# Summing the sample heads' state products: two float32 products with a selector, or two turns on TensorE and a VectorE sum

## The reference, cut to what matters

```python
s = jnp.einsum('bhtd,bhsd->bhts', q, k) * w_ts
decay = jnp.exp(b + m_prev[..., None] - m_t)
num = decay[..., None] * jnp.einsum('bhtd,bhdv->bhtv', q, c_prev) + jnp.einsum('bhts,bhsv->bhtv', s, v)
den = decay * jnp.einsum('bhtd,bhd->bht', q, n_prev) + jnp.sum(s, axis=-1)
h = num / jnp.maximum(jnp.abs(den), jnp.exp(-m_t))[..., None]
...
c_new = carry[..., None, None] * c_prev + jnp.einsum('bhs,bhsd,bhsv->bhdv', g, k, v)
```

## Time and profile before

| what | value |
|---|---|
| median of 3 runs | 1702.03 us |
| the profiled execution, its own time | 1702.65 us |
| its span in the trace | 1700.9 us |
| TensorE matmul busy | 1690.0 us, 99% |
| VectorE busy | 1199.5 us, 71% |
| ScalarE busy | 766.8 us, 45% |
| GpSimd busy | 478.9 us, 28% |
| mean granted TensorE clock | 0.998 of full speed |

### The profile page before, as it was taken

The page is one execution under the profiler, slowest core; times in us unless marked ns, Lnnn a source line. Parts: engine busy times, 40 slices in busy tenths (PEclk is TensorE's granted clock), DMA queues, the critical chain, the costliest instruction groups (busy, mean ns, idle before and its releaser), DMA issues.

```text
span 1700.9 us, 37193 instructions
## 1 busy us (share of the span) xinstructions
PE 1690.0 (99%) x13726; PEld 1683.3 (99%) x13726; DVE 1199.5 (71%) x1901; ACT 766.8 (45%) x916; POOL 478.9 (28%) x501
## 2 busy tenths in 40 slices
PE   9999999999999999999999999999999999999997
PEld 8999999999999999999999999999999999999997
DVE  5875958668495866849688877777555777777554
ACT  6534435454443535444445555544333434334443
POOL 4432515232151523215333222222000222222220
PEclk9999999999999999999999999999999999999999
DMA  8788786868778686877776666666666666666663
GB/s 199 185 232 196 196 215 153 231 164 227 185 201 207 155 232 161 232 181 201 194 183 180 191 176 184 181 178 174 183 181 180 182 179 181 177 181 178 184 176 120
DMA packets 591165, 318.80 MB, mean 187 GB/s; under 512 B 17684, under 2 KB 585988, under 8 KB 588988
## 3 DMA queue, kind: packets, MB, share of 16 engines
q1 hardware_dynamic: 578564, 292.99, 64.0%
q10 hardware_dynamic: 10448, 21.57, 4.7%
q0 software_dynamic: 2064, 2.92, 0.8%
HBM read 305.09 MB, written 12.78 MB: 187 GB/s over the span
## 4 chain that ended last, share of the span: by engine, by line
PE 99%; ACT 0%; POOL 0%; DVE 0%; issue 0%; ACTq 0%; POOLq 0%; DVEq 0%
PE strip L1532 32%; PE strip L1524 32%; PE strip L1528 32%; PE aux L1403 1%; PE aux L1411 1%; PE strip L1455 0%; PE aux L1585 0%; PE aux L1475 0%; PE strip L1468 0%; PE aux L1615 0%; PE aux L1614 0%; PE aux L1628 0%; PE strip L1403 0%; PE aux L1619 0%; PE aux L1620 0%; PE aux L1612 0%
## 5 line engine op out<-in xcount | busy, mean ns | idle before, releaser
L982 DVE TENSOR_TENSOR w_lo<-w_raw,w_hi 128x1024 fp32r<-128x1024 f32 x556 | 720.4, 1299 | 309.3 <-ACT w_hi L713 308.7
L713 ACT ACTIVATE w_hi<-w_raw 128x1024 fp32r<-128x1024 f32 x557 | 586.5, 1059 | 751.8 <-PE strip L1532 710.2
L1524 PE MATMUL strip<-xh,w_hi 128*128 128x268 f32 (+1 forms) x2016 | 291.1, 286 | 0.0
L1532 PE MATMUL strip<-xh,w_lo 128*128 128x268 f32 (+1 forms) x2016 | 290.7, 286 | 0.0
L1528 PE MATMUL strip<-xl,w_hi 128*128 128x268 f32 (+1 forms) x2016 | 290.1, 286 | 0.0
L1532 PEld LDWEIGHTS strip<-xh,w_lo 128*128 128x128 f32 x2016 | 265.2, 188 | 0.4
L1524 PEld LDWEIGHTS strip<-xh,w_hi 128*128 128x128 f32 x2016 | 265.1, 188 | 0.2
L1528 PEld LDWEIGHTS strip<-xl,w_hi 128*128 128x128 f32 x2016 | 265.3, 188 | 0.0
L1524 PE MATMUL strip<-x2h,w_hi 128*128 128x266 f32 x1408 | 200.1, 284 | 0.0
L1528 PE MATMUL strip<-x2l,w_hi 128*128 128x266 f32 x1408 | 199.9, 284 | 0.0
L1532 PE MATMUL strip<-x2h,w_lo 128*128 128x266 f32 x1408 | 199.9, 284 | 0.0
(11 more groups left out here) (330 smaller groups left out, 1529.1 us busy)
## 6 DMA issues: line engine op xcount, KB each, us to landing
w_raw<-in_w_in SPq DMA_DIRECT2D x256, 512.0 KB, 4.5
w_raw<-in_w_up SPq DMA_DIRECT2D x176, 512.0 KB, 4.1
w_raw<-in_w_down SPq DMA_DIRECT2D x64, 512.0 KB, 4.0
w_raw<-in_w_out SPq DMA_DIRECT2D x32, 512.0 KB, 4.4
w_raw<-in_w_down SPq DMA_DIRECT2D x32, 384.0 KB, 3.4
out<-c_st ACTq DMA_DIRECT2D x8, 1024.0 KB, 7.0
c_st<-in_state_mlstm_C ACTq DMA_DIRECT2D x7, 1024.0 KB, 11.2
rb<-scratch_rows ACTq DMA_DIRECT2D x8, 270.0 KB, 5.1
```

The costliest lines, as they stand in the source:

```text
L713: act.activation(w_hi[:, slot, :], w_raw[:, slot, :], ACT.Copy).then_inc(hi_done, 1)
L982: v.tensor_tensor(w_lo[:, slot, :], w_raw[:, slot, :], w_hi[:, slot, :].bitcast(f32), ALU.subtract).then_inc(lo_done, 1)
L1524: pe.matmul(bank[b][:, 0:c1 - c0], w_hi[:, slot, w], rh[:, k0 + k, c0:c1], start=(first and k == 0), stop=False)
L1532: mm = pe.matmul(bank[b][:, 0:c1 - c0], w_lo[:, slot, w], rh[:, k0 + k, c0:c1], start=False, stop=(last and k == kk - 1))
```

## The change

The two products with `sel` become two turns of the halves of `sacc` (128 x 128 each, in one pass) into `aux0` and `aux1`, columns 258 to 385. VectorE then sums the 16 groups with two `tensor_reduce` into `hsum` (128 x 2 x 8) at `i` 22, ahead of the multiplication into `h_t`, and waits for its own two results. `sel`, the instruction that makes it and the semaphore for it are gone. `hsum` has 64 bytes on each partition, `sel` had 32.

```diff
-        sel = sb("sel", [P, NS])
+        hsum = sb("hsum", [P, 2, NS])
...
-            v.tensor_reduce(sel[:, :], ident[:, :].rearrange("p (g b) -> p b g", b=NS), mybir.AxisListType.X, ALU.add)\
-             .then_inc(sel_done, 1)
...
                         v.wait_ge(sample_done, n + 1)
-                        v.tensor_tensor(h_t[:, :, PM:NM], aux[0][:, PM:PM + 2 * NS].rearrange("p (a b) -> p a b", a=2),
+                        for w in range(2):
+                            v.tensor_reduce(hsum[:, w, :], aux[w][:, PM:PM + P].rearrange("p (g b) -> p b g", b=NS),
+                                            mybir.AxisListType.X, ALU.add).then_inc(hsum_done, 1)
+                        v.wait_ge(hsum_done, n * 2 + 2)
+                        v.tensor_tensor(h_t[:, :, PM:NM], hsum[:, :, :],
                                         rden[:, PM:NM].unsqueeze(1).broadcast_to([P, 2, NS]), ALU.mult)\
                          .then_inc(hs_step, 1)
...
-                        pe.wait_ge(sel_done, 1)
                         pe.wait_ge(sacc_step, (n + 1) * (JG + 1))
                         for w in range(2):
-                            mm = pe.matmul(aux[0][:, PM + w * NS:PM + (w + 1) * NS], sacc[:, 0, w * P:(w + 1) * P],
-                                           sel[:, :], start=True, stop=True)
+                            mm = turn(aux[w][:, PM:PM + P], sacc[:, 0, w * P:(w + 1) * P], P)
                         mm.then_inc(sample_done, 1)
```

More of the change, by code:

```diff
@@ L328, in hybrid_decoder_step @@
             sem("scores_done"), sem("kv_turned"), sem("kv_done"), sem("vs_done"), sem("v_kept"))
-        wsc_done, qkd_done, qkd_turned, sn_done, sel_done = (
-            sem("wsc_done"), sem("qkd_done"), sem("qkd_turned"), sem("sn_done"), sem("sel_done"))
+        wsc_done, qkd_done, qkd_turned, sn_done, hsum_done = (
+            sem("wsc_done"), sem("qkd_done"), sem("qkd_turned"), sem("sn_done"), sem("hsum_done"))
         psum_step, n_kept = sem("psum_step"), sem("n_kept")
```

## The result

| | before | after |
|---|---|---|
| median of 6 runs | 1701.86 us (1701.14 to 1702.46) | 1708.51 us (1707.41 to 1709.86) |
| ratio, 95% interval | | 1.0038 (1.0028 to 1.0048) |
| profiled execution, its span | 1702.65, 1700.9 us | 1708.56, 1706.8 us |
| TensorE busy | 1690.0 us | 1695.6 us |
| VectorE busy | 1199.5 us | 1202.0 us |

The time rose by 6.65 us where a fall of 1.8 was forecast, and 1708.51 lies outside the range. The page of the changed kernel still names TensorE for 99% of the chain, as the earlier trace rows did; TensorE is busy 5.6 us longer, with 16 fewer matmuls.

The account below looks back on a forecast made before the run. TensorE was taken to bound the kernel, with 99% of the chain. A saving of 1.8 us with nothing added by VectorE gave 1702.03 - 1.8 = 1700.2 us for the median, range 1698.4 to 1702.8.

Parts of the forecast that it names:

- TensorE's saving: At L1628, two turns replace two float32 products: 0.22 us for 0.45 a head, 1.8 us saved over eight heads.
- VectorE's cost: At `i` 22 of each head, two reduces and the wait for them take 0.8 us, adding nothing on the path.
- The cover: Behind `i` 22, TensorE needs the split for unit 27 only later: 5.6 us of cover against 0.8 us.
- At `i` 16 the waiting: Rival: VectorE's 0.8 us delay reaches `i` 16, which has no cover; seven heads pay, 1705.8 us; chance 0.03.
- Gain given back: Rival: TensorE, 0.23 us earlier at `i` 16, waits longer there in seven heads; 0.2 us gain left, 1701.8; chance 0.07.
- turns at full duration: Rival: the turns do not overlap, a pair takes 0.55 us; 0.8 us lost in all, 1702.8 us; chance 0.06.
- falling clock: Rival: turns don't count as work, so a unit behind them runs at 1.2 GHz; 23.4 us lost, about 1724; chance 0.01.
- The pace behind the turns: Rival: strips behind L1634 take 2.98 us a unit instead of 2.93; 6.3 us lost, 1706.5 us; chance 0.09.
- the 0.13 of slower cases: Combined chance of pace, VectorE's delay and clock making the kernel slower by over 0.2%, above 1705.4 us.

Follow-up runs that it names:

- sums_only: Kernel before with the two VectorE reduces added at `i` 22, their result unused; 1701.89 us beside 1702.3 of the kernel before.
- turns_only: Changed kernel without VectorE's two reduces, so the sum over the 16 groups is left out; 1707.37 us beside 1702.3 of the kernel before.
- turns_last: Changed kernel with the two turns moved behind L1634, right ahead of strip 11; 1703.7 us beside 1702.3 of the kernel before.
- products_too: Changed kernel with two float32 products of 8 columns added behind the turns, into columns nobody reads; 1708.35 us.
- wait_out: Kernel before with its wait for `sel` taken out of the heads and put once ahead of them; 1702.52 us beside 1701.57 of the kernel before.
- before_plus_turn: Kernel before with one turn of half of `sacc`, result unread, ahead of its two products; 1708.38 us beside 1701.57 of the kernel before.
- turns_between: Changed kernel with the two turns between L1633 and L1634; 1704.95 us beside 1701.57 of the kernel before.
- turns_mid: Changed kernel with the two turns ahead of L1624, the last product of the state; 1702.85 us beside 1701.57 of the kernel before.
- mid_tails_first: turns_mid with the last of the seven turns at `s == 4` put first there; 1702.36 us beside 1702.56 of the kernel before, ratio 1.0000.
- mid_scores_last: turns_mid with the three score products at `s == 4` put behind the seven turns; 1702.6 us beside 1702.56 of the kernel before, ratio 1.0002.

## Why the prediction was wrong, point by point

- **TensorE's saving** (0.45 us to 0.22 us a head): right. The loads give 0.22 us, L1633 its 0.12.
- **VectorE's cost** (0.8 us a head, hidden): right in kind, a little high: 0.28 us a reduce where I took 0.4, `cgs` later by 0.71 us. The cover held, and `sums_only` puts the cost at 0.1 us for seven heads. At `i` 16 the waiting did not grow; behind slow strips it went away, which the forecast had not thought of (0.7 us).
- **Gain given back, turns at full duration, falling clock**: none of them. Each turn costs 0.11 us, and the clock is 1.00 in every stretch shown.
- **The pace behind the turns**: here the prediction failed. Its sum left the strips at 2.93 us a unit; they ran at 2.98 behind `s == 10` and behind `s == 4`, 486 more slow groups, 8.0 us against a saving of 1.8. I had seen both paces in the trace of before and given the slower one 0.09. I held two things against it. That L1633 and L1634 stand between turns and strip proves nothing: the changed kernel has them there and is slow. That the matmuls behind the pair of output turns follow at 0.125 us speaks of strips of 264 columns, which took the same times in both kernels (on average 0.968, 0.972 and 0.977 us for eight at the three lines of a unit); that row couldn't tell of 268 columns. The rows that could, showed the pace change behind a single small turn.
- **The size of that rival** (126 units x 0.05 = 6.3 us, time 1706.5): near, but by luck, as it counts the wrong units. The 32 units of the output projection behind the last head stayed fast. In their place come the 12 units behind `s == 4` of heads 1 to 7, which I did not think of, since nothing changes there. Counted: 8.0 us instead of 6.3.
- **The range**: I left the 0.13 of slower cases outside, with the whole of the forecast resting on a saving of 1.8 us, while a cause with 6 us at stake had been seen in the same trace.

What is shown: the turns bring the loss and VectorE's part does not; small edits that hardly change the work move the time by up to 6.8 us; the time follows the count of slow groups. Between the restarts (us; the sum is 0.0165 us for each slow group beyond 66, the work of seven heads, and the late waits less 0.74):

| kernel | measured | slow groups | late waits | change | sum |
|---|---|---|---|---|---|
| before | 697.99 | 66 | 0.74 | | |
| after | 703.31 | 525 | 0 | +5.3 | +5.2 |
| turns_only | 703.31 | 525 | 0 | +5.3 | +5.2 |
| sums_only | 698.07 | 66 | 0.83 | +0.1 | +0.1 |
| turns_last | 699.61 | 251 | 0.71 | +1.6 | +1.4 |
| products_too | 703.01 | 315 | 0 | +5.0 | +4.9 |
| wait_out | 697.68 | 56 | 0.57 | -0.3 | -0.3 |
| before_plus_turn | 703.06 | 342 | 0.46 | +5.1 | +5.0 |
| turns_between | 699.41 | 281 | 0.15 | +1.4 | +1.3 |
| turns_mid | 697.42 | 155 | 0.29 | -0.6 | -0.6 |
| mid_tails_first | 697.98 | 192 | 0.24 | 0.0 | 0.0 |
| mid_scores_last | 698.33 | 190 | 0.21 | +0.3 | -0.1 |

The sums lie within 0.2 us of what was measured, but for `mid_scores_last` (0.4), whose changed order at `s == 4` has a price of its own that the sum leaves out. **What stays open** is why one restart picks the fast pace and the next the slow one. The second distance behind the turns of `s == 4` goes with it in heads 1 to 7, and in three kernels the pace alternates from head to head with the same instructions. So something else than these instructions has a part in it; whether that is carried over from the head before, or lies in the other engines or the DMAs, no run here shows.

## What to carry to other kernels

In a kernel that one engine bounds for 99% of its span, measure the steady distance between the instructions of its longest loop, not only the price of the lines that an edit touches. If the same shape at the same clock is found at two distances, then any edit ahead of that loop carries the difference times the whole loop as a risk on both sides, and this belongs in the range, not outside of it. Run the same edit at two or three places before the saving, or the loss, is put down to the edit itself.

## What the runs showed of the hardware

- Matmuls of 268 columns in a steady stream, each with its own weight load, go at 122.1 or at 124.2 ns on average, both at a granted clock of 1.00, and mostly hold the pace from a break in the stream to the next (up to 36 groups of eight). The break can be a block of small products. It can be the late weight split at `i` 16: behind it six groups were slow in each of five heads of the kernel before, while in `turns_last` the strips stayed fast behind it in four of five heads. It can also be a change of width: the one strip of 268 columns behind the three of 280 (18 groups) is slow in every head of every kernel, and makes 35 of the 66 slow groups of the kernel before.
- 266 columns take 123.3 ns from column 14 of `xh`, 122.5 from column 12, and 121.7 from column 4 of `mh`: fewer columns don't always take less time.
- A float32 product of 8 columns costs TensorE more (0.45 us for two, with the late load behind them) than a turn of 128 x 128 (0.22 us for two).
- A reduce of 128x8 from 128x128 out of PSUM took 280 ns, 381 the one from SBUF at the kernel's start.
